# Heads whose scan carries its own one, a query split shared out anew, and an earlier store of the residual

## The reference, cut to what matters

```
mask = k_pos < q_pos
log_keep = where(mask, log_sigmoid(-z), 0)
later = reversed cumsum(log_keep) - log_keep
a = where(mask, exp(log_sigmoid(z) + later), 0)
out = a @ v
```

## Time and profile before

| | us |
|---|---|
| median of three runs | 873.5 |
| the profiled execution | 875.3 |
| its span, first to last instruction | 873.6 |
| TensorE busy | 819.9 |
| VectorE busy | 566.1 |
| ScalarE busy | 482.1 |
| GpSimd busy | 348.3 |

### The profile page before, as it was taken

One profiled execution on the slowest core, in us unless ns is written; L12 is line 12 of the kernel. 1 busy time (PEld: TensorE's weight loads), 2 busy tenths in 40 slices (PEclk: granted clock), 3 DMA queues, 4 the chain that ended last, 5 costly groups with the idle time before them and its releaser, 6 DMA issues.

```text
span 873.6 us, 14850 instructions
## 1 busy us (share of the span) xinstructions
PE 819.9 (94%) x5001; PEld 573.1 (66%) x5001; DVE 566.1 (65%) x620; ACT 482.1 (55%) x1603; POOL 348.3 (40%) x211
## 2 busy tenths in 40 slices
PE   5999999988999999999999999999979997999995
PEld 3666667766754434444478878777745544899995
DVE  4545375788976777887898654332178996655553
ACT  4611382235676677769986433312288895444433
POOL 3000000966685998686895000000166763011110
PEclk9999999999999999999999999999979999999998
DMA  9999868645689997997998089998887989521302
GB/s 327 380 372 334 320 223 292 218 144 203 219 293 357 395 341 242 332 322 272 395 381 319 1 326 339 365 323 311 309 319 278 333 324 377 210 97 49 98 1 98
DMA packets 109820, 236.79 MB, mean 271 GB/s; under 512 B 7505, under 2 KB 66712, under 8 KB 109488
## 3 DMA queue, kind: packets, MB, share of 16 engines
q1 hardware_dynamic: 51136, 174.29, 54.7%
q10 hardware_dynamic: 58608, 61.54, 21.1%
HBM read 222.54 MB, written 13.27 MB: 270 GB/s over the span
## 4 chain that ended last, share of the span: by engine, by line
PE 55%; DVE 14%; ACT 11%; DMA 10%; issue 4%; POOL 3%; SPq 2%; ACTq 0%; POOLq 0%; DVEq 0%
PE ps L1759 19%; PE ps L1762 8%; PE ps L1746 7%; PE ps L2196 5%; PE ps L1743 4%; DMA slot<-in_cache_k_dram 4%; ACT slot L907 4%; DVE w_lo L1216 2%; PE ps L1723 2%; DMA work<-in_cache_v_dram 2%; POOL slot L641 2%; DMA w_raw<-in_gla_w_in_dram 2%; DVE zall L1402 2%; DVE states L1436 2%; DVE slot L1401 1%
## 5 line engine op out<-in xcount | busy, mean ns | idle before, releaser
L641 POOL TENSOR_TENSOR slot<-slot,qb 128x1024 f32<-128x1024 f32 x97 | 252.4, 2633 | 100.5 <-DMA slot<-in_cache_k_dram 63.0
L1402 DVE TENSOR_REDUCE zall<-slot 128x16 f32<-128x1024 f32 x97 | 116.9, 1215 | 28.1 <-POOL slot L641 27.0
L1216 DVE TENSOR_TENSOR w_lo<-w_raw,w_hi 128x1024 fp32r<-128x1024 f32 x57 | 82.2, 1443 | 78.5 <-ACT w_hi L736 78.3
L907 ACT ACTIVATE slot<-slot 128x64 f32<-128x64 f32 x496 | 119.3, 244 | 18.9 <-POOL slot L641 18.9
L736 ACT CAST w_hi<-w_raw 128x1024 fp32r<-128x1024 f32 x58 | 60.7, 1047 | 73.7 <-PE ps L1762 36.8
L907 ACT ACTIVATION_READ_ACCUMULATOR slot<-slot 128x1 f32 x496 | 94.3, 190 | 0.0
L1746 PE MATMUL ps<-xn,w_raw 128*128 128x512 f32 x192 | 85.4, 596 | 1.7 <-ACT xn L747 1.7
L1746 PE MATMUL ps<-xn,w_unsplit 128*128 128x512 f32 x192 | 83.7, 593 | 0.0
L1762 PE MATMUL ps<-xa_hi,w_hi 128*128 128x512 f32 x200 | 81.7, 409 | 1.7 <-DVE w_lo L1216 1.7
L1759 PE MATMUL ps<-xb_hi,w_hi 128*128 128x260 f32 x384 | 78.9, 287 | 1.1 <-DVE w_lo L1216 0.9
L1762 PE MATMUL ps<-xa_hi,w_lo 128*128 128x512 f32 x200 | 79.2, 396 | 0.0
(11 more groups left out here) (326 smaller groups left out, 1508.0 us busy)
## 6 DMA issues: line engine op xcount, KB each, us to landing
slot<-in_cache_k_dram SPq DMA_DIRECT2D x128, 512.0 KB, 6.2
slot<-in_cache_v_dram SPq DMA_DIRECT2D x120, 512.0 KB, 6.0
w_raw<-in_gla_w_in_dram ACTq DMA_DIRECT2D x12, 1024.0 KB, 7.3
slot<-in_gla_w_in_dram SPq DMA_DIRECT2D x24, 512.0 KB, 9.5
w_raw<-in_w_kv_dram ACTq DMA_DIRECT2D x8, 1024.0 KB, 11.2
w_raw<-in_w_ple_gate_dram ACTq DMA_DIRECT2D x6, 1024.0 KB, 5.3
s<-in_state_gla_dram SPq DMA_DIRECT2D x1, 4096.0 KB, 22.3
out_dram<-s ACTq DMA_DIRECT2D x4, 1024.0 KB, 8.7
```

The costliest lines, as they stand in the source:

```text
L641: nc.gpsimd.tensor_tensor(slot[s][:], slot[s][:], qb[:, (n // NPG) % 2, :], ALU.mult).then_inc(S("k_mul_pool"), 1)
L907: ins = nc.scalar.activation(part, part, ACT.Copy, accum_out=zall[:, n % NPG, b * SH + h:b * SH + h + 1])
L1216: nc.vector.tensor_tensor(lo, raw, hi.bitcast(F32), ALU.subtract).then_inc(S("w_split"), 1)
L1402: nc.vector.tensor_reduce(zall[:, n % NPG, b * SH:(b + 1) * SH], at.rearrange("p (h d) -> p h d", d=HD), AX.X, ALU.add).then_inc(S("k_used ...
```

## The change

The scan gets `ident` as its mask at the query's own block: the state starts at zero, becomes one at the query itself and is multiplied on from there. Keys from the query on then have zero weight through `pcum`, so the select on `psig` goes; only the last column of each query block, whose product reads the next block's first column, is set to zero (`cut_ends`). Since a scan must now start at each query block's own end, there are four scans a head in place of three. ScalarE makes one copy of the query's high part; GpSimd subtracts and then makes the other copy (`query_split`), for head h + 2 when the first bank of head h has its sigmoids and before it cuts head h. ScalarE's copies run one head further ahead. The residual's store moves from i = 8 to i = 5; the first key tile then also waits until the last reader of `hT` is done. At the heads' start, ScalarE's sigmoids of head 0 come after value tile 14, VectorE's `sample_gate(1)` before the scans of head 0, and TensorE's page group 16 ahead of value tile 15's transposes.

```diff
-        passed = at("passed", [P, NP_TOK + P], F32, off_sqacc + 2 * P * 4)
+        passed = at("passed", [P, NP_TOK], F32, off_sqacc + 2 * P * 4)
...
-            def query_low(h):
+            def query_split(h):
+
+                z = qz[h % 4]
                 pool.wait_ge(S("qz"), h + 1)
-                nc.gpsimd.tensor_tensor(z[r, 1, :], q1T[r, h // 2, :], z[r, 0, :].bitcast(F32), ALU.subtract).then_inc(S("q_low"), 1)
-                pool.wait_ge(S("q_low"), h + 1)
+                nc.gpsimd.tensor_tensor(z[own_half(h), 1, :], q1T[own_half(h), h // 2, :], z[own_half(h), 0, :].bitcast(F32),
+                                        ALU.subtract).then_inc(S("q_low"), 1)
+                pool.wait_ge(S("q_low"), 2 * h + 1)
+                nc.gpsimd.tensor_copy(z[other_half(h), 0, :], z[own_half(h), 0, :].bitcast(F32)).then_inc(S("q_low"), 1)
+                pool.wait_ge(S("q_low"), 2 * h + 2)
...
+            nc.gpsimd.memset(passed[:, 0:NP_TOK - P], 0.0)
+            nc.gpsimd.tensor_copy(passed[:, NP_TOK - P:NP_TOK], ident[:]).then_inc(S("masks"), 1)
...
+            def cut_ends(h):
 
                 A = psig[h % 2]
+                pool.wait_ge(S("sig_p"), (h + 1) * len(ZBANKS))
+                nc.gpsimd.memset(A[:, 3 * P - 1:4 * P:P], 0.0)
+                nc.gpsimd.memset(A[:, 6 * P - 1:10 * P:4 * P], 0.0).then_inc(S("sig_cut"), 1)
+
+            pool.wait_ge(S("masks"), 4)
+            for h in range(2, 4):
+                query_zero(h)
             for h in range(SH):
-                cut_causal(h)
                 if h + 2 < SH:
-                    pool.wait_ge(S("sig_cut"), h + 1)
-                    if h < 2:
-                        query_zero(h + 2)
-                    query_low(h + 2)
+                    if h:
+                        pool.wait_ge(S("sig_cut"), h)
+                    pool.wait_ge(S("sig_p"), h * len(ZBANKS) + 1)
+                    query_split(h + 2)
+                cut_ends(h)
...
                 if t == 0:
                     act.wait_ge(S("h_moved"), 16)
+                    act.wait_ge(S("x_ready"), (X_SPLIT.index(4) + 1) * KT)
...
-                q = q1T[own_half(h), h // 2, :]
-                nc.scalar.copy(qz[h % 4][own_half(h), 0, :], q)
-                nc.scalar.copy(qz[h % 4][other_half(h), 0, :], q).then_inc(S("qz"), 1)
+                nc.scalar.copy(qz[h % 4][own_half(h), 0, :], q1T[own_half(h), h // 2, :]).then_inc(S("qz"), 1)
...
-                if i == 8:
-                    act.wait_ge(S("x_ready"), (X_SPLIT.index(4) + 1) * KT)
+                if i == 5:
+                    act.wait_ge(S("h_new"), KT)
+                    act.wait_ge(S("s_h"), 3)
                     act.dma_start(h_rows, hT[:, :, :]).then_inc(S("h_moved"), 16)
...
                     query_high(1)
-                    head_sigmoids(0)
                 if i >= KV_LAG + 8:
                     kv_tile(i - KV_LAG - 8)
+            head_sigmoids(0)
...
             kv_sample_rows(1)
+            query_high(4)
...
-                if h + 4 < SH:
-                    query_high(h + 4)
+                if h + 5 < SH:
+                    query_high(h + 5)
...
-                for e, (bk, cols, _) in enumerate(ZBANKS):
+                for e, (_, _, blocks) in enumerate(ZBANKS):
                     dve.wait_ge(S("sig_p"), h * len(ZBANKS) + e + 1)
-                    s, m = ZSEG[bk], PASSED[bk]
-                    rev = C[:, s + cols - 1:s - 1 if s else None:-1]
-                    held = passed[:, m + cols - 1:m - 1 if m else None:-1]
-                    own.did(nc.vector.tensor_tensor_scan(rev, rev, held, 1.0, ALU.mult, ALU.max))
+                    for q in blocks:
+                        n, s = (q + 1) * P, PSEG[q]
+                        rev = C[:, s + n - 1:s - 1 if s else None:-1]
+                        at_query = passed[:, NP_TOK - 1:NP_TOK - n - 1 if n < NP_TOK else None:-1]
+                        own.did(nc.vector.tensor_tensor_scan(rev, rev, at_query, 0.0, ALU.mult, ALU.max))
...
             sample_rows(1)
+            sample_gate(1)
             head_scans(0)
-            sample_gate(1)
...
+            value_quad(QUAD * 16)
             for t in range(16 - KV_LAG, 16):
                 kv_transposes(t)
...
-            value_quad(QUAD * 16)
```

More of the change, by code:

```diff
@@ L114 @@
 ZSEG = {0: 0, 1: 512, 2: 768}
-PASSED = {0: P, 1: 2 * P, 2: 0}
 NZ = P * (1 + 2 + 3 + 4)
@@ L268, in build @@
         rstd = new("rstd", [P, T])
-        passed = at("passed", [P, NP_TOK + P], F32, off_sqacc + 2 * P * 4)
-        assert off_sqacc + (2 * P + NP_TOK + P) * 4 <= top[0]
+        passed = at("passed", [P, NP_TOK], F32, off_sqacc + 2 * P * 4)
+        assert off_sqacc + (2 * P + NP_TOK) * 4 <= top[0]
         ident = new("ident", [P, P])
@@ L656, in query_zero @@
                 pool.wait_ge(S("qz_zero"), h + 1)
-            def query_low(h):
-                z, r = qz[h % 4], own_half(h)
+            def query_split(h):
+                z = qz[h % 4]
                 pool.wait_ge(S("qz"), h + 1)
-                nc.gpsimd.tensor_tensor(z[r, 1, :], q1T[r, h // 2, :], z[r, 0, :].bitcast(F32), ALU.subtract).then_inc(S("q_low"), 1)
-                pool.wait_ge(S("q_low"), h + 1)
+                nc.gpsimd.tensor_tensor(z[own_half(h), 1, :], q1T[own_half(h), h // 2, :], z[own_half(h), 0, :].bitcast(F32),
[3 more added lines that the diff above has]
+                pool.wait_ge(S("q_low"), 2 * h + 2)
@@ L665, in _ @@
             for h in range(2):
                 query_zero(h)
-                query_low(h)
+                query_split(h)
             own.wait()
             pool.wait_ge(S("evac"), last_tile("V"))
[L671 to L676, removed]
@@ L678, in cut_causal @@
-            def cut_causal(h):
-                A = psig[h % 2]
[L681 to L691, removed]
+            nc.gpsimd.memset(passed[:, 0:NP_TOK - P], 0.0)
@@ L2141, in scores @@
                     pe.wait_ge(S("evac"), last_tile("V"))
-                pe.wait_ge(S("q_low"), h + 1)
+                pe.wait_ge(S("q_low"), 2 * h + 2)
                 pe.wait_ge(S("qz_zero"), min(h + 1, 4))
```

## The result

The changed kernel takes 878.0 us (median of nine runs, 875.17 to 879.04); the kernel before, run beside it, 874.04 us (nine runs, 872.85 to 877.85). The recorded ratio is 1.0034, 95% interval 1.0019 to 1.005: slower, by more than the 0.2% that a measurement tells from no change. (It is not the quotient of the two medians, which is 1.0045.) The profiled execution took 878.0, its span 876.3. The forecast was 874.9 within 870.0 to 878.5, with "slower" at 0.42; the rival named *slower* gave 877.3.

A forecast was written before the change was run, and what follows sets the result against it. VectorE, the TensorE-ScalarE loop and the page ring were taken to bound pairs, all at 11.7 to 12.4 us. Start +1.4, pairs 0, store 0 on a profiled 875.3, less 1.8 to the median, gave 874.9; range 870.0 to 878.5.

The forecast's parts named there:

- rival *slower: Scans from head 2: subtract and copy hold them fully; +1.4 start, +1.7 pairs, +0.7 head 9, 877.3 us; chance 0.22.
- VectorE's 12.0 to 12.6 a pair: Steady pairs: VectorE's scans, products, gate and time shut out by GpSimd's subtract and copy, against 12.03 us before.
- the 12.0 case: Steady pairs: the even head's subtract runs under the PSUM-reading gate, hiding its 0.60, so VectorE takes 12.0 us.
- the split's price on the scans: Each head's scans: GpSimd's subtract holds VectorE back by up to 1.12 us, its copy by 0.45.
- so its 11.7 holds for all pairs: Steady pairs: the TensorE-ScalarE loop, read from heads that copy no more queries, takes 11.7 us in every pair.
- pairs under 11.8: Steady stage: pairs shorter than 11.8 us were listed as a sign that the prediction is wrong.
- the page ring's 12.4: TensorE's page slots: one turn of four slots takes 12.4 us, and two such sets serve a pair.
- for the sum I take the pairs as they were, 12.3: Pairs with splits from head 4: kept at 12.3 us, between 11.7 and 12.6; change 0, bounds -3.3 to +1.7.
- +1.4 on entry: Start of the heads: later sigmoids, split and head 0 product delay the steady stage 1.4 us, bounds 0 and +2.5.
- The store: Residual's store three gates earlier: gain zero, at most the 2.0 us that TensorE idles in the key and value stage.
- rival *start not late: Start of the heads: the early page group keeps TensorE busy at full clock, pairs unchanged; 873.5 us, chance 0.10.
- rival *faster: Steady pairs: scans leave GpSimd room, VectorE falls to 10.0, loop's 11.7 remains; 871.6 or 870.2 us, chance 0.20.

The follow-up runs named there:

- scans_alone: The kernel before with only the new mask, four scans and column cut; split stays behind the cut, ScalarE makes both query copies: 873.87 us, ratio 0.9987.
- split_after_9: The changed kernel with GpSimd's split of head 11's queries held back until head 9's product is done: 875.09 us, ratio 0.9996.
- rows_early: The changed kernel with VectorE's sample rows ahead of head 9's scans and sample gate ahead of its product: 873.94 us, ratio 0.9987.
- copy_on_scalar: The changed kernel with the second query copy back on ScalarE, GpSimd only subtracting: 875.52 us, ratio 1.0007.
- best_quad_early: best_guess with TensorE's page group 16 put back ahead of value tile 15's transposes: 875.7 us, ratio 1.0026.
- best_guess: The changed kernel with sample rows and gate before head 9's scans and product, head 0 cut before head 2's split, old heads' start: 871.89 us, ratio 0.9959.
- best_sigmoids_late: best_guess with ScalarE's sigmoids of head 0 put back behind value tile 14: 873.4 us, ratio 1.0004.

## Why the prediction was right, and where not

The direction held, and 878.0 lies in the stated range. But it lies outside the forecast's own 873.0 to 876.7; it is in the range because that took in the rivals' prices. And that the rival *slower* came within 0.7 us is luck: its terms were 1.4 for the start, 1.7 for the pairs and 0.7 for head 9, and the trace has 0.53, -2.3 and 5.5.

**Bounds of the steady stage: half right.** VectorE's 12.0 to 12.6 a pair with the split beside the scans came out as 12.29 and, a little below it, 11.74 (the second with its subtract under the gate, as the 12.0 case had it). Scans (3.0 forecast, 2.96 measured), product (1.49), GpSimd's copy (0.65, measured 0.62) and the split's price on the scans (1.57, measured 1.45) were right; the copy's share of it, 0.45, measured 0.41 (4.42 less 4.01), though 1.12 of 1.27 would make it 0.57. The loop of TensorE and ScalarE, "so its 11.7 holds for all pairs", came out at 11.55, and at 11.87 with ScalarE's second copy back: "pairs under 11.8", a sign of being wrong, came up. Nor did the page ring's 12.4 bind there: TensorE waited for no page in the three pairs at 11.55.

**The step that failed is "for the sum I take the pairs as they were, 12.3".** With one number for a pair, an engine at 11.55 and one at 12.3 make a stage of 12.3. In fact TensorE ran at 11.55 for three pairs on the slack that I had named ("some 2 us between an even head's product and its transposes"), and when the samples' rows came up, 1.6 us of VectorE's work once in the heads, what was left of it did not cover head 9's stretched scans: of the 1.83 us by which the rows lost ground there, 0.63 was slack already lost and 1.20 head 9's own split. The six pairs from head 2 to 14 averaged 12.76 after, 12.23 before. The mechanism was the rival *slower*, whose condition held at head 4, where the subtract (662.69) began with the first scan and not under the gate, though not at heads 6 and 8. It had the place too ("0.7 at head 9, whose product the subtract missed before"), but as the price of one stretched product. It measured 5.5, because TensorE waits for VectorE there twice and then pays the clock for it. The forecast of 874.9 lies 3.1 below the measured 878.0.

**The start: the working right, the rest too large.** Sigmoids behind value tile 14, the split ahead of the cut, the product late, TensorE's transposes 2.2 late (2.14), ScalarE's taking of them 0.6 to 1.8 late (1.64): all as worked out. Of the +1.4 on entry only 0.53 was left at head 2, within the bounds of 0 and 2.5: in the kernel before TensorE waited another 3.4 us between head 0 and head 2 (0.9, 0.5 and 2.0, all for ScalarE), in the changed kernel 1.8. Page group 16 had not landed when TensorE came to it early (1.26 of waiting).

**The store: right.** Zero within 0.3 us in the value stage: from K's first product (500.52 before, 498.79 after) to V's end TensorE took 131.5 and 131.8. That V ended at 630.60, more than 0.5 from 632.0 and so a sign of being wrong by the prediction, comes from the stages ahead. That the rival *start not late* and the rival *faster* fell is plain from the rows; the freed VectorE of the latter exists in scans_alone, but there pages and the loop hold the pairs at 11.96 to 12.9, as its counter-argument said.

**What made it slower, shown:** the stall at heads 8 and 9, which needs a split beside head 9's scans (split_after_9), the samples' rows behind them (rows_early), and a VectorE that has lost part of its lead: copy_on_scalar has a subtract beside the scans, the rows behind them and no stall. That the lead counts is read from the times in these traces; no kernel changes it alone. **Not settled:** why best_quad_early costs 0.67% of ratio, what the early page group costs with the gate ahead of head 0's scans, and how much of best_guess's lead would repeat. Not tried: scans_alone with GpSimd's copy of the query and the rows moved, which would have VectorE's room and the 11.55 loop at once.

## What to carry to other kernels

When two engines go at different rates, don't take the slower one's period for the stage at once: look for the slack that the faster one lives on, how much of it each turn takes, and which rare piece of work needs more than is left; and count what stretches the work just ahead of that piece, here the larger part (1.20 of 1.83 us). Work that another engine waits for goes ahead of long work in an engine's queue, above all where a neighbour's instruction can stretch that long work. And work moved beside an instruction that it shuts out is not hidden by it; put it beside one that it leaves alone, as the gate is here (0.69 with a subtract beside it, 0.68 without), or behind.

## What the runs showed of the hardware

A short wait costs more than its length when TensorE's clock falls after it: after waits of 1.56 and 2.28 a page group of 1.92 took 3.64 at 0.50, and even the transposes behind it 2.06 in place of 1.31. At the heads' end the same happened in some kernels and not in others, for 1.7 us: after waits of 1.80 and 1.94 the group ran at 0.57 (best_sigmoids_late), and after 1.54 and 1.95 too (scans_alone), while the kernel before kept its full clock after 2.14 and 1.86 and the changed one after 1.93 and 1.99. The length of these waits alone does not decide it.

Between VectorE and GpSimd, the instruction that began first held back the other, even when it was only 0.07 us ahead: the subtract that began at 697.36 held back the product at 697.43 (2.57 in place of 1.49), while subtracts that began behind a product took up to 2.26 in place of 1.27.
